# Strip pairs of an MLP: a fifth unit by seven products, low parts over the loaded weights, twelve cells for high parts

## The reference, cut to what matters

```python
def squared_relu_mlp(x, w1, w2):          # x 256 x 2048, w1 2048 x 8192, w2 8192 x 2048
    h = jax.nn.relu(x @ w1)
    return (h * h) @ w2
```

## Time and profile before

| | us |
|---|---|
| median of 3 runs (2122.4 to 2124.38) | 2122.74 |
| the profiled execution's own time | 2122.97 |
| its span, first to last instruction | 2121.2 |

### The profile page before, as it was taken

The page is one execution under the profiler, slowest core; times in us unless marked ns, Lnnn a source line. Parts: engine busy times, 40 slices in busy tenths (PEclk is TensorE's granted clock), DMA queues, the critical chain, the costliest instruction groups (busy, mean ns, idle before and its releaser), DMA issues.

```text
span 2121.2 us, 26630 instructions
## 1 busy us (share of the span) xinstructions
PE 2098.9 (99%) x9860; PEld 1751.8 (83%) x9860; DVE 1596.4 (75%) x1623; ACT 1055.1 (50%) x1196; POOL 25.6 (1%) x38
## 2 busy tenths in 40 slices
PE   9999999999999999999999999999999999999998
PEld 7888887888888888888888888888888888888886
DVE  6766666859788788696687767577686977978876
ACT  5445656435445354453645544555354554544543
POOL 2000000000000000000000000000000000000001
PEclk9999999999999999999999999999999999999999
DMA  9554564666566566666464555554666655656563
GB/s 286 180 177 159 173 244 161 216 217 220 180 213 220 198 209 209 227 227 238 159 220 158 182 177 177 174 185 161 230 203 228 212 195 198 236 196 214 204 228 149
DMA packets 216122, 426.18 MB, mean 201 GB/s; under 512 B 14993, under 2 KB 50049, under 8 KB 215025
## 3 DMA queue, kind: packets, MB, share of 16 engines
q1 hardware_dynamic: 214208, 415.75, 58.1%
q0 software_dynamic: 1840, 9.44, 1.3%
HBM read 406.26 MB, written 2.10 MB: 193 GB/s over the span
## 4 chain that ended last, share of the span: by engine, by line
PE 87%; DVE 3%; SPq 3%; DMA 3%; issue 2%; ACT 1%; POOL 0%; DVEq 0%; POOLq 0%
PE ps L1017 18%; PE ps L1019 17%; PE ps L1018 17%; PE ps L929 10%; PE ps L955 6%; PE ps L957 5%; PE ps L956 5%; PE ps L933 5%; SPq L379 3%; DMA raw<-in_mlp_w 1%; DMA raw<-in_ev_w_in 1%; PE ps L1130 0%; DVE res L1517 0%; DVE w_lo L1926 0%; DVE late L1951 0%
## 5 line engine op out<-in xcount | busy, mean ns | idle before, releaser
L790 ACT ACTIVATE w_hi<-raw 128x1024 fp32r<-128x1024 f32 x284 | 294.9, 1058 | 317.8 <-PE ps L1019 312.6
L1422 DVE TENSOR_TENSOR w_lo<-raw,w_hi 128x1024 fp32r<-128x1024 f32 x264 | 319.6, 1219 | 127.9 <-ACT w_hi L498 127.1
L1919 DVE TENSOR_TENSOR w_lo<-raw,w_hi 128x1024 fp32r<-128x1024 f32 x284 | 342.5, 1219 | 88.9 <-ACT w_hi L790 88.7
L498 ACT ACTIVATE w_hi<-raw 128x1024 fp32r<-128x1024 f32 x256 | 267.5, 1056 | 170.4 <-PE ps L957 113.8
L1017 PE MATMUL ps<-w_hi,yT 128*128 128x512 f32 x812 | 316.3, 390 | 0.0
L1019 PE MATMUL ps<-w_hi,yT 128*128 128x512 f32 x812 | 316.0, 389 | 0.0
L1018 PE MATMUL ps<-w_lo,yT 128*128 128x512 f32 x812 | 315.9, 389 | 0.0
L929 PE MATMUL ps<-xT,w_hi 128*128 128x512 f32 x1016 | 259.0, 396 | 2.1 <-DVE xT L1467 1.0
L929 PEld LDWEIGHTS ps<-xT,w_hi 128*128 128x128 f32 x1016 | 183.1, 188 | 36.7 <-issue 1.5
L1017 PE MATMUL ps<-w_hi,xT 128*128 128x512 f32 x524 | 204.8, 391 | 2.8 <-DVE res L1517 2.4
L1018 PE MATMUL ps<-w_lo,xT 128*128 128x512 f32 x524 | 203.9, 389 | 0.0
(11 more groups left out here) (273 smaller groups left out, 3248.2 us busy)
## 6 DMA issues: line engine op xcount, KB each, us to landing
raw<-in_mlp_w SPq DMA_DIRECT2D x256, 1024.0 KB, 5.2
raw<-in_od_w_in SPq DMA_DIRECT2D x48, 1024.0 KB, 5.1
raw<-in_ev_w_in SPq DMA_DIRECT2D x36, 1024.0 KB, 5.1
raw<-in_ev_w_out SPq DMA_DIRECT2D x16, 1024.0 KB, 5.1
raw<-in_od_w_out SPq DMA_DIRECT2D x16, 1024.0 KB, 5.1
ks<-cross SPq DMA_DIRECT2D x256, 32.0 KB, 1.9
ks<-qs SPq DMA_DIRECT2D x256, 32.0 KB, 1.9
raw<-in_ev_w_in SPq DMA_DIRECT2D x8, 512.0 KB, 8.8
```

Of the source, the lines that this page charges most:

```text
L498: nc.scalar.activation(flat(w_hi[:, k % NSPL]), flat(raw[:, k % NRAW]), ACT.Copy).then_inc(s_hi, 1)
L790: nc.scalar.activation(slot_part(0, slot, 2), flat(raw[:, k % NRAW]), ACT.Copy).then_inc(s_hi, 1)
L1422: nc.vector.tensor_tensor(flat(w_lo[:, k % NSPL]), flat(raw[:, k % NRAW]), flat(w_hi[:, k % NSPL]).bitcast(F32), ALU.subtract).then_inc(s_ ...
L1919: nc.vector.tensor_tensor(slot_part(1, slot, 2), flat(raw[:, k % NRAW]), slot_part(0, slot, 2).bitcast(F32), ALU.subtract).then_inc(s_lo, 1)
```

## The change

- The units become `"SSOSOSSO"`: five of eight by seven products, the first two units among them. The order of x tiles over the units changes with it. The x sums of the fifth unit are made in the layer's first pair, a second batch, and their high and low parts are kept in tiles of `xT` that are needed no more.
- Low parts of weights are written over the loaded weights themselves (`raw_lo` has the address of `raw`), and those of the weight sums over the sums. The room of all slots, high and low, goes to twelve cells for high parts. A load now waits until the chunks in its place are multiplied (`s_used`), not until their low parts are made.
- SyncE's exchanges are issued in parts of 4 and 8 between loads, not 16 at once.
- TensorE begins a pair step with an S unit: its plain products wait for the addition of bank pair 4, 5, and its summed products for that of 6, 7. The copied product bank is 4, no longer 6.
- The orders of ScalarE and VectorE are written anew for five S units. In the last two blocks of a layer the low parts go to `w_lo` as before.

The units, the room and the queue of SyncE:

```diff
-UNITS = "OSOSOSSO"
-KT_PAIR = (0, 4, 1, 5, 2, 6, 7, 3)
+UNITS = "SSOSOSSO"
+KT_PAIR = (4, 5, 0, 6, 1, 7, 3, 2)
-NRING = 6
+NCELL = 12
+N_FIRST = 4
+N_LATER = NS - N_FIRST
+SKIPS = (DOWN + 2, DOWN + 4, DOWN + 6, DOWN + 8, DOWN + 10, DOWN + 12)
...
+        raw_lo, late_lo = sb("raw_lo", [P, NRAW * CK * CN], F32R), sb("late_lo", [P, 2048], F32R)
+        more_hi, rg_lo = sb("more_hi", [P, 4 * S * 4], F32R), sb("rg_lo", [P, 2 * 4 * S], F32R)
...
+                def load_used(blk, q, until, src):
+
+                    sp.wait_ge(s_used, (blk - 1) * BLK + until)
+                    sp.dma_start(raw[:, 2 * q:2 * q + 2].rearrange("p k t c -> p (k t) c"), src).then_inc(s_raw[q], 16)
+
+                def up_unit(blk, u, pairs, p):
+                    q = u % PAIRS
+                    load_used(blk + u // PAIRS, q, 2 * q + 1 if 0 <= u - PAIRS in SUMMED and pairs > 1 else 2 * q + 2,
+                              w_pair[layer][KT_PAIR[u], pairs:PAIRED][p])
...
-                        if v == 2 * PAIRS - 2:
+                        if v == 4:
                             sp.wait_ge(s_block_tr, pair * 2 + (h0 + 1))
-                            move_hidden(0)
+                            move_hidden(0, 0, 4)
+                        if v == 5:
+                            move_hidden(0, 4, 8)
+                        if v == 6:
+                            move_hidden(0, 8, 16)
...
                     for u in range(2 * PAIRS):
-                        up_unit(blk, i + 2, u)
-                        if u == 0:
+                        up_unit(blk, u, 2, i)
+                        if u == 2:
                             sp.wait_ge(s_sq, i * 2 + (h0 + 3))
-                            move_hidden(1)
+                        if 2 <= u < 6:
+                            move_hidden(1, 4 * u - 8, 4 * u - 4)
```

ScalarE in a layer's first pair:

```diff
+                    if k == DOWN:
+                        act.wait_ge(s_sums, 8 * layer + 8)
+                        act.wait_ge(s_used, blk * BLK + DOWN)
+                        nc.scalar.activation(cells_hl[0][:, 0:4 * N_LATER], late_sums.rearrange("p (n s) -> p n s", s=P),
                                              ACT.Copy).then_inc(s_sum_hi, 1)
```

TensorE in a pair step:

```diff
                             if first:
-                                pe.wait_ge(s_sum_lo, layer + 1)
+                                pe.wait_ge(s_sum_lo, 2 * layer + 2)
+                                pe.wait_ge(s_added, i * 4 + (n0 + 3))
+                            plain_products(blk, u, turn, first, last)
+                            if first:
                                 pe.wait_ge(s_added, i * 4 + (n0 + 4))
-                            plain_products(blk, u, first, last)
                             summed_products(blk, u, first, last)
```

VectorE, two helpers and the head of its order in a pair step:

```diff
+                def plain_lo(blk, u, turn):
+
+                    dve.wait_ge(s_plain_hi, turn * NS + (SUMMED.index(u) + 1))
+                    dve.wait_ge(s_wsum, turn * (3 * NS) + (3 * SUMMED.index(u) + 3))
+                    nc.vector.tensor_tensor(lo_part(2 * u, 1, 3), raw_unit(2 * u)[:, CN:4 * CN],
+                                            hi_part(RING_CELL[2 * u], 3).bitcast(F32), ALU.subtract).then_inc(s_plain_lo, 1)
...
+                        if e >= 2:
+                            dve.wait_ge(s_used, blk * BLK + (2 * SUMMED[e - 2] + 2))
...
+                    sums(0, 0)
+                    add_down(blk, i, 2, -4)
+                    sums(0, 1)
+                    sums(0, 2)
+                    plain_lo(blk, 0, turn)
                     sums(1, 0)
+                    summed_lo(blk, 0)
                     sums(1, 1)
                     sums(1, 2)
+                    add_down(blk, i, 3, 0)
+                    plain_lo(blk, 1, turn)
+                    summed_lo(blk, 1)
+                    sums(3, 0)
+                    lo(4)
+                    sums(3, 1)
+                    lo(5)
+                    sums(3, 2)
+                    plain_lo(blk, 3, turn)
+                    summed_lo(blk, 3)
...
```

More of the change, by code:

```diff
@@ L374, in mlp, with move_hidden @@
             def mlp(layer, b0):
[L375 to L386, removed]
+                def move_hidden(buf, first, last):
+                    for n in range(first, last):
+                        a, c = divmod(n, NQ)
+                        sp.dma_start(tiles_moved[QUAD * c:QUAD * c + QUAD, :, a],
+                                     turned_in[buf][QUAD * a:QUAD * a + QUAD, c]).then_inc(s_moved, 16)
@@ L388, in mlp, with down_unit, down @@
+                def down_unit(blk, p, v, summed=True):
+                    q = v % PAIRS
+                    load_used(blk + v // PAIRS, q, 2 * q + 1 if summed and v + PAIRS in SUMMED else 2 * q + 2,
+                              w_m2[layer][p * 2 + v % 2, v // 2])
                 h0 = FB * layer
-                def down(blk, p, pair):
+                def down(blk, p, pair, summed=True):
                     for v in range(2 * PAIRS):
-                        down_unit(blk, p, v)
-                        if v == 2 * PAIRS - 2:
+                        down_unit(blk, p, v, summed)
+                        if v == 4:
@@ L1234, in wide_chunk @@
                         for half in range(2):
-                            hi, lo = (slot_block(h, slot, half) for h in range(2))
-                            ins = three_products(ps[:, WIDE_BANKS[half] + tok], cells(kt, tok), hi, lo, start, stop)
+                            bank = WIDE_BANKS[half] + tok
+                            ins = three_products(ps[:, bank], cells(kt, tok), hi_block(cell, half), lo_part(k, half, 1),
+                                                 bank in starts, stop)
@@ L1262, in down @@
-                def down(blk, k, pair, slot, src=hT):
+                    three_products(ps[:, 1], cells(kt + 1, 1), *t_4, first, False).then_inc(s_used, 1)
+                def down(blk, k, pair, w, src=hT):
                     nb, quarter = divmod(k, 4)
@@ L1324, in mlp @@
                         pe.wait_ge(s_added, n0 + 4 * (PAIRED - 1) + k // 4 - 1)
-                    down(blk, k, ((4, 5), (6, 7))[k // 4 % 2], k % NSPL, hT_last)
+                    down(blk, k, ((4, 5), (6, 7))[k // 4 % 2], [(w_hi[:, k % NSPL, i], w_lo[:, k % NSPL, i]) for i in range(CK)], hT_last)
                 if n_end == 4:
@@ L2077, in pair_step @@
                     join_products(turn, 4)
-                    for k in range(DOWN + 2, DOWN + 6):
-                        lo(k)
+                    lo(DOWN + 2)
+                    lo(DOWN + 3)
                     dve.wait_ge(s_used, blk * BLK + DOWN)
```

346 lines of the change are left out of this document (193 added, 153 removed).

## The result

The changed kernel takes **2108.76 us** (median of 4 runs, 2108.57 to 2109.86) where the one before takes 2122.61 in the same series (4 runs). The ratio is 0.9935, 95% interval 0.9921 to 0.9949: 13.85 us less. The forecast was 2109.5, in a range of 2107.5 to 2116. The profiled execution took 2109.86 us, with a span of 2108.0.

The account below looks back on a forecast made before the run. TensorE, busy 99% of the span, was taken as the bound, so time comes from fewer products or closed gaps. Terms -8.2, -6.3 and +1.0 sum to -13.5 us, from 2122.97 to 2109.5; range 2107.5 to 2116.

Parts of the forecast that it names:

- Fifth unit: Fifth seven-product unit: three products fewer in each of 12 pair steps, 36 x 0.2267 us, 8.2 us less.
- The wait on the addition: TensorE's wait near a pair step's start on VectorE's residual addition of bank pair 6, 7 closes: 6.3 us less.
- VectorE's load: VectorE's added work in a pair step, about 73 of 83.7 us busy, hidden beside products: costed at nothing.
- The layout: Times of VectorE's work in the new pair step, counted from its first product; least slack 1.4 us.
- Low parts over the weights: Low parts written over loaded weights make loads wait for multiplied chunks; loads still land in time: costed at nothing.
- The rival of a late load: Unit 3's load lands after 7.0 us and stalls TensorE; 2.0 us lost per step would give 2133; 7%.
- Exchanges in parts: SyncE's issues in parts of 4 and 8 push no load past its deadline, last blocks included: costed at nothing.
- First pair: In each layer's first pair, chunk 17 of the down phase waits on a low part: 1.0 us more, bounds 0 and 2.
- The sum: Whole kernel: -8.2 - 6.3 + 1.0 = -13.5 us, from 2122.97 to 2109.5 us.
- the second rival: VectorE falls behind at unit 1 or 3, losing 0.6 us per step: 2116.5 us; 9%.

Follow-up runs that it names:

- the order alone: Kernel before, with VectorE's addition of bank pair 6, 7 put first and the squaring moved behind unit 1's summed low part: 2119.61 us, ratio 0.9984.

## Why the prediction was right

**Fifth unit: right.** -8.2 forecast; three products put back cost 8.2. The distance of starts was the price; the mean duration of 0.39 us would have given 14. The sustained gap of about 131 ns, which the Trainium skill ("TensorE: Matmul & The Clock Gate", Back-to-back issue gap) states, would have given an estimated 4.7; these products do not come so close.

**The wait on the addition: right in what the change does, incomplete in its cause.** -6.3 forecast, 6.6 us of gaps closed over ten steps (849.8 - 836.4 less 30 products), and the margin was as small as said. (The forecast has 6.5 us of gaps and takes 6.3; it gives no working for the difference.) But it put all 6.5 us down to the one wait that the profile names, where 0.7 of them were at the next latecomer, "the low part of unit 1". And it told the cause as VectorE's order in the step ("it had squaring and two low parts ahead of it"), without asking why VectorE began that work so late: it had idled 8.4 us for a load behind the sixteen pieces. With the order alone the old place is closed, if the squaring is moved too, and 2.9 of the 6.5 us come back at units 3 and 6; had the change been the order alone, the same working would have missed by nearly half. It came out right here because it laid out the new kernel as a whole, its loads and exchanges included, and that layout held. What would split the 2.9 further was not tried: exchanges in parts in the kernel before, four seven-product units on the new buffers, or five on the old slots.

**VectorE's load: right.** 73.6 us in a step of 83.64 (about 73 forecast). The layout held to about 1 us: unit 1's low parts ended at T + 3.1 and 5.3 (3.2 and 5.4 forecast), unit 6's summed one at 30.6 (29.5, needed at 32.0). No step was lost:

```profile
649.73:733.37 83.64, 83.64 (x371) 69.28 (x370) 73.62 (x64) 40.84 (x37) 0.00 (x0) 1.00 0.64 213
```

**Low parts over the weights: right.** Unit 3's load was ready at T + 5.9 where 5.5 was forecast, its chunk 4 at 8.3 where 7.8 was, both inside the slack. The rival of a late load did not come.

**Exchanges in parts: "nothing" was 0.6 us, and the step that failed is the landing time.** In the pair steps nothing was the right cost, but the parts are no neutral term either: with an exchange at once TensorE's waits add to 43.5 or 24.7 us. In the last blocks they cost 0.54 and 0.1 us. The prediction held that the pieces "do not queue for long", from their median of 1.9 us in the earlier trace rows, where sixteen were issued in a row. Between loads of 1 MB it was 4.2, and the last one of the second half, which is the one that counts, took 2.5: SyncE's timeline has that half's eight issues of 0.63 us from 973.06 on, the last near 977.5, and the squaring started at 980.10.

```profile
973.06 5.06 SPq L410 DMA_DIRECT2D ks<-qs  x8
```

The product that needs the addition was due at 982.11. Against it the half was issued by -4.0 in place of -4.5, landed 0.6 later than 1.9 allows, and the squaring and addition ended at -0.8 and +0.35 in place of -2 and -0.9. The layout had 0.9 us of margin, less what TensorE needs between the addition's end and its product, and 1.25 came on top. The Trainium skill ("DMA: Bandwidth & Descriptors", Queues, rings and completion order) says that each DMA engine consumes descriptors in ring order; that pieces with a load of 1 MB just ahead of them land later agrees with it. The prediction used the rule for a load behind pieces and not for pieces behind a load.

**First pair: right.** 1.0 us forecast, 1.1 measured, at the chunk and for the cause named.

**The sum.** -13.5 forecast, -13.85 measured by medians and -13.2 by spans. What the parts differ by is within the spread of the runs (2107.86 to 2109.87 for the changed kernel). One slip did not matter: the second rival is put at 2116.5 and counted into a range that ends at 2116.

## What to carry to other kernels

Price a product by the distance of starts, and a wait by the time between products, not by the wait that the profile names: where several things become ready together, removing the named one shows the next, and the whole gap goes only when all of them are early. Follow the late engine back to its last idle time as well: here that was a load behind an exchange, 11 us ahead of the wait that showed. Lay out the engine's order after the edit down to the last instruction ahead of the deadline, each with its duration. In a queue that issues in order, small transfers stand in the way of large ones by their count of issues, so split them between the loads, and take their landing time from a stretch where they have loads ahead of them.

## What the runs showed of the hardware

**A long wait costs more than itself.** Where TensorE stood for 1.8 to 4.1 us in a stream of products, the granted clock behind it was often 0.50 (1.2 GHz) for some us: in 8 of the 12 steps of the run with the addition behind both low parts, in 11 with the second exchange at once, in 4 with the first. In the run with the second exchange at once, two stretches behind a wait (columns as above):

```profile
850.80:856.80 6.00, 6.00 (x14) 4.75 (x15) 5.58 (x5) 3.59 (x3) 0.00 (x0) 0.50 0.29 117
856.90:870.00 13.10, 13.10 (x59) 10.83 (x58) 12.55 (x12) 6.57 (x6) 0.00 (x0) 1.00 0.45 160
```

Fourteen products in 6.0 us are 0.43 each, against 0.22 in the second row. In the run with the first exchange at once it differs from step to step. The first of these stretches lies behind a wait of 1.85 us, the second behind one of 1.83:

```profile
742.00:744.00 2.00, 2.00 (x10) 1.68 (x9) 2.00 (x2) 2.00 (x2) 0.00 (x0) 1.00 1.01 403
...
828.00:830.00 2.00, 2.00 (x7) 1.52 (x6) 1.55 (x1) 1.89 (x2) 0.00 (x0) 0.50 1.00 379
```

Two waits of the same length, and only one cost the clock: the wait's length alone does not decide. The waits of 43.5 us cost 67.5, those of 33.3 cost 49.6, and with the first exchange at once 24.7, with 2.8 more that the profile puts down to issue, cost 37.0: 1.3 to 1.6 times the wait (single runs). The clock makes up most of the surplus: in the 6 us behind a wait 26 products start where it stayed at 1.00 and 19 or 20 where it fell (14 in some steps with the second exchange at once), so a fall costs some 1.6 us, an estimate from these counts. Eight of them are 13 of the 16 us by which 49.6 exceeds 33.3. The small waits of the kernel before left the granted clock at 1.00 in the stretch of the earlier trace rows. The Trainium skill ("TensorE: Matmul & The Clock Gate", Part 1: The HAM clock gate) says that the clock is set by how busy the array has recently been; that it falls behind a wait agrees with it. Why one of two equal waits is spared, these rows do not show. The expectations of these three runs left it out, and the times came out above them.
